# Where SBUF tiles begin: multiples of 256 bytes in place of 32, for the tiles that TensorE streams as fp32r

## What is computed

```python
proj = x @ w_in                      # gates | z | xBC | dt | q_a | kv_a
xbc, conv_new = _causal_conv(xbc, conv_state, conv_w, conv_b)
yh, s_fin = _ssd(xh, dt, a, bm, cm, s0, chunk)       # state-space scan, 8 groups of 4 heads
y_ssm = (_rmsnorm(yg) * ssm_norm_g) @ w_ssm_proj
q = (_rmsnorm(q_a) * q_norm_g) @ w_q_b
o = _mla_attend(q_nope, q_pe, ckv, kpe, w_uk, w_uv, q_pos, k_pos)
y_mla = o @ w_mla_proj
mix = (g_ssm * y_ssm + g_mla * y_mla) @ w_out
h = _layernorm(ALPHA * x + mix, ln1_g, ln1_b)
ff = jnp.square(jax.nn.relu(h @ w_up)) @ w_down
y = _layernorm(ALPHA * h + ff, ln2_g, ln2_b)
```

## Time and profile before

| | |
|---|---|
| median of the runs | 827.81 us |
| profiled execution | 827.16 us |
| its span, first to last instruction | 825.0 us |
| TensorE busy | 97% |
| VectorE busy | 72% |
| ScalarE busy | 58% |
| GpSimd busy | 10% |
| granted TensorE clock, mean | 0.995 |
| moved by DMA | 123.32 MB, 149 GB/s |

### The profile page before, as it was taken

One profiled execution on the slowest core, in us unless ns is written; L12 is line 12 of the kernel. 1 busy time (PEld: TensorE's weight loads), 2 busy tenths in 40 slices (PEclk: granted clock), 3 DMA queues, 4 the chain that ended last, 5 costly groups with the idle time before them and its releaser, 6 DMA issues.

```text
span 825.0 us, 15682 instructions
## 1 busy us (share of the span) xinstructions
PE 797.6 (97%) x6347; PEld 767.2 (93%) x6347; DVE 590.5 (72%) x974; ACT 478.5 (58%) x828; POOL 84.9 (10%) x174
## 2 busy tenths in 40 slices
PE   5999999999999999999999999999999999999994
PEld 5998999899899898888999999999999999999993
DVE  5796956746745758798888988666688887755554
ACT  5694855755656568544666546434457887633432
POOL 0214111111102002000000000000000000001212
PEclk9999999999999999999999999999999999999997
DMA  8457335335336225343443444555555554555541
GB/s 300 141 184 284 113 127 163 111 107 175 104 102 183 78 92 160 114 124 123 151 145 126 147 136 133 201 176 160 172 155 155 168 163 162 170 154 175 159 127 58
DMA packets 34088, 123.32 MB, mean 149 GB/s; under 512 B 4192, under 2 KB 4336, under 8 KB 33760
## 3 DMA queue, kind: packets, MB, share of 16 engines
q1 hardware_dynamic: 30816, 110.67, 42.6%
q0 software_dynamic: 3008, 10.98, 3.8%
q10 hardware_dynamic: 192, 0.66, 0.2%
HBM read 118.26 MB, written 4.04 MB: 148 GB/s over the span
## 4 chain that ended last, share of the span: by engine, by line
PE 72%; DVE 14%; ACT 9%; issue 3%; DMA 1%; ACTq 0%; DVEq 0%
PE ps_acc L427 13%; PE ps_acc L428 12%; PE ps_acc L429 12%; DVE wlo L1292 3%; PE ps_row L428 3%; PE ps_row L429 3%; PE ps_row L427 3%; ACT whi L900 2%; PE ps_cb L428 2%; PE ps_tr L428 2%; PE ps_tr L429 2%; PE ps_cb L429 2%; PE ps_tr L427 2%; PE ps_cb L427 2%; DVE seg L1579 2%
## 5 line engine op out<-in xcount | busy, mean ns | idle before, releaser
L1292 DVE TENSOR_TENSOR wlo<-wraw,whi 128x1024 fp32r<-128x1024 f32 x204 | 248.9, 1222 | 165.3 <-ACT whi L900 165.0
L900 ACT CAST whi<-wraw 128x1024 fp32r<-128x1024 f32 x204 | 213.3, 1046 | 123.9 <-DMA wraw<-in_wst 123.3
L427 PE MATMUL ps_acc<-xh,whi 128*128 128x288 f32 x576 | 177.0, 307 | 10.1 <-DVE wlo L1292 8.4
L428 PE MATMUL ps_acc<-xl,whi 128*128 128x288 f32 x576 | 171.0, 297 | 0.0
L429 PE MATMUL ps_acc<-xh,wlo 128*128 128x288 f32 x576 | 170.8, 297 | 0.0
L427 PEld LDWEIGHTS ps_acc<-xh,whi 128*128 128x128 f32 x576 | 109.4, 190 | 18.2 <-DVE wlo L1292 8.4
L428 PEld LDWEIGHTS ps_acc<-xl,whi 128*128 128x128 f32 x576 | 109.5, 190 | 0.5
L429 PEld LDWEIGHTS ps_acc<-xh,wlo 128*128 128x128 f32 x576 | 109.4, 190 | 0.0
L1351 DVE SCALAR_TENSOR_TENSOR cv<-xp,vec,cv 128x292 f32<-128x292 f32 x96 | 50.1, 522 | 7.9 <-ACT cv L965 5.5
L427 PE MATMUL ps_acc<-o_h,whi 128*128 128x288 f32 x128 | 39.4, 308 | 0.0
L428 PE MATMUL ps_acc<-o_l,whi 128*128 128x288 f32 x128 | 37.7, 295 | 0.0
(11 more groups left out here) (444 smaller groups left out, 2250.8 us busy)
## 6 DMA issues: line engine op xcount, KB each, us to landing
wraw<-in_wst SPq DMA_DIRECT2D x204, 512.0 KB, 3.5
side<-in_ukT POOLq DMA_DIRECT2D x8, 256.0 KB, 3.7
side_v<-in_ukT POOLq DMA_DIRECT2D x8, 256.0 KB, 3.4
out_ssm<-s_out POOLq DMA_DIRECT2D x8, 256.0 KB, 2.6
x<-in_xT SPq DMA_DIRECT2D x2, 576.0 KB, 4.8
ax<-in_xT POOLq DMA_DIRECT2D x1, 1152.0 KB, 6.0
out_y<-d SPq DMA_DIRECT2D x4, 288.0 KB, 2.1
ckvT<-in_cacheT POOLq DMA_DIRECT2D x1, 1024.0 KB, 7.1
```

What stands on the lines that cost most here:

```text
L427: pe.matmul(out, w, mh, start=first, stop=False)
L428: pe.matmul(out, w, ml, start=False, stop=False)
L900: act.copy(whi[:, s % RING, :], wraw[:, s % RING, :]).then_inc(split_hi, 1)
L1292: tt(wlo[:, s % RING, :], wraw[:, s % RING, :], whi[:, s % RING, :].bitcast(F32), ALU.subtract).then_inc(split_lo, 1)
```

## The change

The constant LINE = 256 is added. `base` and `here` round up to it in place of 32. `after` rounds up to it for tiles of type fp32r, and to 32 as before for all others. No instruction, order, semaphore or size is changed; only the addresses of tiles are.

```diff
@@ -36,6 +36,7 @@
 RING = 5
+LINE = 256
 CK = 1024
@@ -155,7 +156,7 @@
-        base = (nc.sbuf_base + 31) // 32 * 32
+        base = (nc.sbuf_base + LINE - 1) // LINE * LINE
@@ -167,10 +168,11 @@
         def after(name, shape, dt=F32):
-            return at(name, shape, (end[0] + 31) // 32 * 32, dt)
+            line = LINE if dt == F32R else 32
+            return at(name, shape, (end[0] + line - 1) // line * line, dt)
 
         def here():
-            return (end[0] + 31) // 32 * 32
+            return (end[0] + LINE - 1) // LINE * LINE
```

## The result

The changed kernel takes 829.32 us, the median of eight runs (828.82 to 830.37), the kernel before 826.90 us in the runs taken beside it. The ratio is 1.0029, with a 95% interval of 1.0019 to 1.0038. The forecast was 813.0, between 808 and 828, worked from the first three of those runs (827.81); the time went the other way by 2.4 us.

A forecast was written before the change was run, and what follows sets the result against it. TensorE's matmul start-to-start distances were taken as the bound. 16.6 us gross less 2.2 not reaching the end gave 14.4 net; 827.16 - 14.4 = 812.8, or 813.4 from the median, put at 813.0, range 808 to 828.

The forecast's parts named there:

- What bounds the kernel: Whole kernel: TensorE's start-to-start distances of matmuls set the time, with TensorE busy 797.6 of 825.0 us.
- the cover in the groups: Eight state-space groups: one dense chunk each before the transposes saves nothing, as VectorE was already last; 0.9 us.
- the six tiles: xh, q_h, ckv_h, ff_h, mix_h and o_h: every slot would begin and end on a multiple of 128.
- I therefore read the difference as a cost of a moving stream that does not begin and end on a multiple of 128: 288-column products: aligned slots would take 127.5 ns in place of 132.2, 15.8 us less over 3,360 matmuls.
- the 16.6 us: Gross gain forecast: 15.8 us from 288-column matmuls and 0.8 from ckv's, before 2.2 us that would not reach the end.
- The key projection's 4.3 ns less: Key projection, moving ckv at 256 columns: 192 matmuls would each save 4.3 ns, 0.8 us.
- The stationary operand doesn't explain it: Decay rows cost 117 ns with one stationary column, so the moving operand's place was held to set the price.
- The value projection's bounds, 0 and +0.8 us: Value projection: 192 matmuls moving from 128 to 0 were taken to change nothing, at worst +0.8 us.
- its bounds: Up projection, 768 matmuls at 290 columns: change taken as 0, between -4.7 and +1.0 us.
- Slower: moving and stationary operand on the same grid get in each other's way: Rival on weights and moving tiles both at 0 or 128: 834 to 842 us, chance 0.12.
- Placement is not it: Rival: the value projection is cheap for something other than its start; 827 us, range 825.4 to 829, chance 0.20.
- The rule that was weighed: SBUF has 16-byte cachelines, so a start on 32 equals one on 256: gain 0, time 827 us.

The follow-up runs named there:

- w64_m64: The changed kernel with both the weight ring and the moving fp32r tiles 64 past a multiple of 256: 829.71 us, ratio 1.0032.
- base256: The kernel before with its base alone on a multiple of 256, so every tile moves by 128: 826.96 us, ratio 0.9997.
- w64_m0: The changed kernel with the weight ring 64 past a multiple of 256, moving fp32r tiles left on multiples: 826.74 us, ratio 0.9994.
- bcast_down: The changed kernel with each stationary operand of the down projection cut to one column read for all 128: 829.23 us, one run.
- ckv_pitch_w64: The changed kernel with weights at 64 and slots of ckv_h and ckv_l 320 columns apart in place of 288: 827.75 us, ratio 1.0007.
- down256: The kernel before, addresses kept, with the down projection over 256 of its 288 columns: 814.18 us, one run, against 826.44 beside it.
- altw: The changed kernel with weights at 64 and each chunk's eight blocks laid to alternate between two places mod 256: 831.58 us, ratio 1.0059.
- bcast_kv: The changed kernel with the stationary operand of the key and value projections cut to one column; value projection 113.3 and 120.0 ns, no whole time given.

## Why the prediction was wrong

**What bounds the kernel** was right. TensorE's distances set the time, the counts of matmuls were right, and the cover in the groups worked, though for a loss: the group stage grew by 0.1 us and L713's wait shrank from 6.0 to 5.4. The addresses of the six tiles and the weights were right. Two details were not. The last byte now is 226,400 (cm ends behind wb), which changes nothing. And e does not walk through all residues: its eight slots, 8 bytes further each mod 128, cover 64 to 120 in e_h and 0 to 56 in e_l before, and 0 to 56 in both after. So the change did move e against the weights, and its rate with it.

**"I therefore read the difference as a cost of a moving stream that does not begin and end on a multiple of 128"** is the step that failed. It rested on one cheap row, 113.3, and turned a correlation over three starts into a cause; it carried all of the 16.6 us. The runs showed another cost in its place: the distance mod 128 between the stationary and the moving operand, 133.2 ns at 0 (the changed kernel and w64_m64) and 132.2 to 132.3 at 64 (the kernel before, base256, w64_m0). w64_m0 has every stream of the six tiles on a multiple of 128, and 132.3 ns, not 127.5. Nor is 113.3 the price of a place: the same places gave 113.3 and 117.8. The key projection's 4.3 ns less came out as 1.1 more on the mean (1.4 in the run shown).

**"The stationary operand doesn't explain it"** was the other half of it. I argued that the decay rows, with a one-column operand, cost 117 like the key projection. That shows that the stationary read does not make the 117. It does not show that two full reads cannot meet at a worse distance, and bcast_down shows that they do: 1.0 ns.

**The value projection's bounds, 0 and +0.8 us**, were too narrow: 113.3 to 119.0 is 5.7 ns, x 192 = 1.1 us more. The up projection, at -0.8 ns on the mean, lies within its bounds.

**The sum that came.** Taken over all matmuls of a tile (mean distance between starts, those above 150 ns left out as waits), the rise is 0.75 ns for x and o, 1.0 for q, 1.05 for ff, 0.9 for mix: 2,112 x 0.75 + 288 x 1.0 + 768 x 1.05 + 192 x 0.9 = 2.9 us. To it come 1.1 for the value projection, 0.2 for the key projection (117.1 to 118.2), 0.3 for yn (131.9 to 132.6), and -0.6 from the up projection (134.5 to 133.6): 3.8 us in all. From the first key projection to the end of TensorE's work the profiled executions show 2.7 us. Of the missing 1.1, 0.8 is in the group stage, whose chunks on x and o should have cost 0.9 and cost 0.1; the wait for btok, where VectorE is last in both kernels, gave back 0.6 of it. The medians show 2.4 us. The distance mod 128 accounts for the 2.9 us of the six tiles. It does not account for the value projection (see ckv_pitch_w64) nor for yn, whose slots meet the same distances before and after, in another order, and still cost 0.7 ns more.

**The rivals.** "Slower: moving and stationary operand on the same grid get in each other's way" named what happened, with its decider: above 132.2 in the down projection. I gave it 0.12 and priced it at 2.3 ns, from e's row; it was 1.0, so the time was 829 and not 835, outside its 834 to 842 too. My argument against it, that the value projection pays less at 128 under 64/192, was none: that is distance 64, where the two reads do not meet. "Placement is not it" described the bulk: some ten of the twelve ns are the moving read, and no place tried took them off.

**The rule that was weighed.** By the Trainium skill, SBUF — State Buffer, section "Door 1: The DMA port swizzle (why `[64,N]` ≈ `[32,N]`)", cachelines are of 16 bytes and an access that crosses to a new one pays. I had worked out from it that a start on a multiple of 32 does as well as one on 256, so 827 us. The runs agree that the larger grid brings nothing (132.2 ns before, 132.3 in w64_m0), but not that starts on the 32-grid are alike: 132.1 to 134.4 by the distance of two operands, and 829.3 us. There the measurement decides.

## What to carry to other kernels

- A cheap row beside dear ones is a lead, not a price. Before scaling it to thousands of matmuls, ask what else differs, and build the one kernel that gives the dear rows only the supposed advantage.
- Look at every round before averaging. The mean of 116.7 ns hid that one round of four ran at 113.3.
- To learn what an operand's read costs, cut it to one broadcast column and keep everything else: three short kernels told 1.0 ns (meeting) from 10.7 ns (moving read), where eleven placements had only shown that nothing helps.
- If fp32r weights and activations both stream all the time, do not align them to the same multiple without a look. Here 64 bytes between them mod 128 were worth 0.3%, and alignment by itself nothing.

## What the runs showed of the hardware

- An fp32r matmul of 288 columns follows the last after 122.5 ns with its moving operand broadcast, and after 132 ns at best with real rows, at a granted clock of 1.00 in both. 256 columns: 116.8 in a long run (down256).
- With the stationary read whole, the down projection goes by the distance between stationary and moving operand mod 128: 133.2 ns at 0, 134.4 at 32 (133.3 in its first block), 132.3 at 64 (up to 133.0 in altw), 132.1 at 96. A common shift of 128 (base256) or 64 (w64_m64 against the changed kernel) changes none of it.
- A stream of 256-column matmuls with the same SBUF addresses can settle at different rates and keep them over a chunk: 113.3 and 120.0 ns in the value projection of bcast_kv, 113.3 and 117.8 in the key projection of ckv_pitch_w64. What picks the rate is open. Other kernels that change only when the stream starts could tell; they were not tried.
- The rate of 290-column slots is 133.4 to 136.0 ns by placement, and dearest when all slots start on a multiple of 256 with weights at 64. Why is open too.
